# Rotary partners moved by DMA and ScalarE, and two modulation blocks summed on VectorE

## What is computed

```
mod = silu(c) @ w_mod + b_mod            # shift1, scale1, gate1, shift2, scale2, gate2
h = rms_norm(x, g1) * (1 + scale1) + shift1
(a_q, a_k, a_v, a_qi, a_ki, a_w, b_u, b_v, c_q, ..., d_q, d_k, d_v) = split_cols(h @ w_in)
q_a, k_a = rope(heads(a_q), pos), rope(heads(a_k), pos)
# rope: [x1*cos - x2*sin, x2*cos + x1*sin], x1 and x2 the halves of a 64-wide head
... four token mixers A (top-k softmax), B (gated MLP), C (forgetting), D (stick-breaking) ...
x = x + gate1 * (merged @ w_out)
h = rms_norm(x, g2) * (1 + scale2) + shift2
x = x + gate2 * conv_ffn(h)              # up, causal conv, silu * val, down
```

## Time and profile before

| | |
|---|---|
| median of 3 runs | 1100.61 us (1099.63 to 1100.64) |
| profiled execution | 1100.77 us, span of the trace 1099.0 us |
| TensorE busy | 1070.9 us (97%) |
| VectorE, ScalarE, GpSimd busy | 574.0, 601.3, 699.9 us |
| DMA | 214.95 MB, mean 196 GB/s |

### The profile page before, as it was taken

One profiled execution on the slowest core, in us unless ns is written; L12 is line 12 of the kernel. 1 busy time (PEld: TensorE's weight loads), 2 busy tenths in 40 slices (PEclk: granted clock), 3 DMA queues, 4 the chain that ended last, 5 costly groups with the idle time before them and its releaser, 6 DMA issues.

```text
span 1099.0 us, 22903 instructions
## 1 busy us (share of the span) xinstructions
PE 1070.9 (97%) x8188; PEld 979.9 (89%) x8188; DVE 574.0 (52%) x1363; ACT 601.3 (55%) x1112; POOL 699.9 (64%) x319
## 2 busy tenths in 40 slices
PE   5999999999999999999999999999999999999996
PEld 2887788898899999999998777889899999999996
DVE  4557743555267755553247576344626685555112
ACT  3564456445446665655456545554545776656542
POOL 0874545445567887778877444545557788777882
PEclk9999999999999999999999999999999999999999
DMA  9955467766654454445566546774534435444541
GB/s 358 362 212 197 186 231 281 235 232 227 199 180 159 148 183 163 153 165 180 191 210 246 209 177 229 252 255 155 189 119 154 154 132 185 176 157 153 191 166 73
DMA packets 85694, 214.95 MB, mean 196 GB/s; under 512 B 13336, under 2 KB 33376, under 8 KB 85360
## 3 DMA queue, kind: packets, MB, share of 16 engines
q1 hardware_dynamic: 85616, 213.88, 55.4%
HBM read 208.80 MB, written 5.05 MB: 195 GB/s over the span
## 4 chain that ended last, share of the span: by engine, by line
PE 85%; DVE 10%; ACT 2%; DMA 2%; issue 1%; SPq 1%; DVEq 0%; POOL 0%; ACTq 0%
PE ps L720 11%; PE ps L716 11%; PE ps L717 11%; PE ps L755 10%; PE ps L756 9%; PE ps L757 9%; PE ps L652 4%; PE ps L708 2%; PE ps L707 2%; PE ps L706 2%; PE ps L1120 2%; PE ps L646 1%; DVE scr L1770 1%; DVE hup L1690 1%; PE ps L861 1%
## 5 line engine op out<-in xcount | busy, mean ns | idle before, releaser
L596 POOL TENSOR_TENSOR wlo<-raw,whi 128x1024 fp32r<-128x1024 f32 x282 | 675.6, 2401 | 347.9 <-ACT whi L1214 290.0
L1214 ACT ACTIVATE whi<-raw 128x1024 fp32r<-128x1024 f32 x202 | 211.6, 1054 | 83.2 <-PE ps L720 62.6
L755 PE MATMUL ps<-hh,whi 128*128 128x288 f32 x816 | 250.6, 307 | 0.8 <-ACT gb L1296 0.8
L756 PE MATMUL ps<-hl,whi 128*128 128x288 f32 x816 | 241.6, 296 | 0.0
L757 PE MATMUL ps<-hh,wlo 128*128 128x288 f32 x816 | 241.3, 296 | 0.0
L755 PEld LDWEIGHTS ps<-hh,whi 128*128 128x128 f32 x816 | 153.7, 188 | 39.0 <-issue 36.2
L717 PE MATMUL ps<-ol,whi 128*128 128x290 f32 x576 | 156.9, 297 | 0.0
L716 PE MATMUL ps<-oh,whi 128*128 128x290 f32 x576 | 156.7, 297 | 0.0
L756 PEld LDWEIGHTS ps<-hl,whi 128*128 128x128 f32 x816 | 153.9, 189 | 0.2
L757 PEld LDWEIGHTS ps<-hh,wlo 128*128 128x128 f32 x816 | 153.7, 188 | 0.0
L716 PEld LDWEIGHTS ps<-oh,whi 128*128 128x128 f32 x576 | 108.9, 189 | 0.0
(11 more groups left out here) (264 smaller groups left out, 1907.0 us busy)
## 6 DMA issues: line engine op xcount, KB each, us to landing
raw<-stream SPq DMA_DIRECT2D x228, 512.0 KB, 4.2
mraw<-stream SPq DMA_DIRECT2D x40, 1024.0 KB
raw<-stream SPq DMA_DIRECT2D x88, 128.0 KB, 5.0
raw<-stream SPq DMA_DIRECT2D x24, 384.0 KB, 5.4
first<-mod_first SPq DMA_DIRECT2D x16, 512.0 KB, 11.6
raw<-stream SPq DMA_DIRECT2D x28, 256.0 KB, 5.2
o_proj<-proj SPq DMA_DIRECT2D x12, 288.0 KB
kvk<-keys_t SPq DMA_DIRECT2D x6, 512.0 KB, 6.4
```

Source lines behind the costliest of these rows:

```text
L596: nc.gpsimd.tensor_tensor(wlo[:, slot, :], raw[:, slot, :], whi[:, slot, :].bitcast(F32), ALU.subtract).then_inc(lo_ready, 1)
L755: mm(out, whi[:, slot, w], high, start=(i == 0), stop=False)
L756: mm(out, whi[:, slot, w], low, start=False, stop=False)
L1214: A(whi[:, slot, :], raw[:, slot, :], ACT.Copy).then_inc(hi_ready, 1)
```

## The change

- The swaps n = 3 to 6 leave TensorE. For each, SP issues four DMAs, which copy 32 partitions by 288 columns each from `proj` to a free slot of `gb`, the halves of each head exchanged (`move_partners`). ScalarE copies the result to PSUM bank 4, 2, 6 or 7 (`take_partner`), at the beginning of its steps t = 18, 19, 21 and 22. `rotate` is as before. In SP's list the copies stand behind piece `in_no(t) + 8` (23, 24, 25 and 26), after that piece's `load_mod` if it has one.
- TensorE's waits for the rotations change: `turn_rows` at t = 19 waits for four rotations (before: five), the logits at t = 20 for five, and the wait for all seven moves from t = 22 to t = 23.
- Two blocks of layer 1's modulation (four pairs, 4 MB) are multiplied in layer 0's down stage on VectorE. The loads stand in SP's list, one ahead of the output stage and three between down pieces, for which SP's loop is written out in the down stage of layer 0. After down tiles 1 to 4 VectorE multiplies one pair: eight instructions of 512 columns, with sums in PSUM banks 2 and 3. In layer 1 TensorE sums the partitions with four matmuls ahead of its first own pair, and layer 1 has 12 pairs instead of 16 (those at t = 32, 34, 36 and 38 are gone).

```
-SWAP_AT = {4: (0, 1, 2), 17: (3,), 18: (4,), 20: (5,), 21: (6,)}
-SWAP_BANK = (4, 3, 5, 4, 4, 4, 4)
+SWAP_AT = {4: (0, 1, 2)}
+PARTNER_AT = {18: 3, 19: 4, 21: 5, 22: 6}
+SWAP_BANK = (4, 3, 5, 4, 2, 6, 7)
+SIDE_LOADS = {8: (1,), 12: (2,), 14: (3,)}
...
+                def move_partners(n):
+                    t = ROPED[n]
+                    sp.wait_ge(bank_free[in_no(t) % 2], taken(l, in_no(t) // 2 + 1))
+                    for r in range(0, P, 64):
+                        for a, b in ((r, r + 32), (r + 32, r)):
+                            sp.dma_start(gb[a:a + 32, n, :], proj[b:b + 32, t, :]).then_inc(partner_loaded[n - ROPED_EARLY], 16)
...
                     if q in after:
                         load_mod(after[q])
+                    for n in range(ROPED_EARLY, len(ROPED)):
+                        if q == in_no(ROPED[n]) + 8:
+                            move_partners(n)
...
+                    sp.wait_ge(mod_read, upto(l, mod_read))
+                    load_side(0)
+                    out_rounds(S_DOWN)
+                    down_pairs()
...
+                def add_side_blocks():
+                    pe.wait_ge(side_turn, 8 * SIDE_BLOCKS)
+                    for g in range(4):
+                        row = 2 * (MOD_B_PAIRS // 2 - SIDE_BLOCKS + g // 2) + g % 2
+                        i = mm(ps[32 * g:32 * g + 32, MOD_BANK, :], one_pad[:, 31 - row:63 - row], side_sums[:, g // 2, g % 2, :],
+                               start=True, stop=True, skip_group_check=True)
...
-                        pe.wait_ge(roped, upto(l, roped, 5))
+                        pe.wait_ge(roped, upto(l, roped, 4))
                         turn_rows(DV, 3, v_turned)
                     if t == 20:
                         pe.wait_ge(v_tok, upto(l, v_tok, 1))
+                        pe.wait_ge(roped, upto(l, roped, 5))
                         prompt_logits(D_ROWS, 0, DQ, DK)
                     if t == 22:
-                        pe.wait_ge(roped, upto(l, roped))
                         turn_probs(D_ROWS, 0)
                         prompt_logits(D_ROWS, 1, DQ, DK)
                     if t == 23:
+                        pe.wait_ge(roped, upto(l, roped))
                         values(D_ROWS, 0)
...
+                def take_partner(n):
+                    act.wait_ge(partner_loaded[n - ROPED_EARLY], upto(l, partner_loaded[n - ROPED_EARLY]))
+                    if n == 3:
+                        act.wait_ge(vb_tok, upto(l, vb_tok))
+                    elif n == 4:
+                        act.wait_ge(scored, upto(l, scored))
+                    else:
+                        act.wait_ge(ol_ready, upto(l, ol_ready, 2))
+                    A(ps[:, SWAP_BANK[n], 0:T], gb[:, n, :], ACT.Copy).then_inc(swapped, 1)
...
+                def add_side_pair(i):
+                    dve.wait_ge(side_loaded[i % 2], 16 * (i // 2 + 1))
+                    for c in range(4):
+                        k = 4 * (i % 2) + c
+                        w = side_pair(i)[:, c // 2, c % 2 * 512:(c % 2 + 1) * 512]
+                        if k:
+                            dve.wait_ge(side_turn, 8 * (i // 2) + k)
+                        for g in range(2):
+                            total = ps[:, 2 + g, :]
+                            by = cpad[:, 32 * k + 30 + g:32 * k + 31 + g]
+                            if k == 0:
+                                s = V.tensor_scalar(total, w, by, None, ALU.mult)
+                            else:
+                                s = V.scalar_tensor_tensor(side_sums[:, i // 2 % 2, g, :] if k == KT - 1 else total, w, by, total,
+                                                           ALU.mult, ALU.add)
+                        s.then_inc(side_turn, 1)
```

More of the change, by code:

```diff
@@ L246, in encoder @@
         fal, _, n2 = place("fal", [P, FT, CC], F32R, at=proj_at + n)
-        hup, _, n3 = place("hup", [P, KT, CC], F32, at=proj_at + n + n2)
+        hup, hup_at, n3 = place("hup", [P, KT, CC], F32, at=proj_at + n + n2)
         assert n + n2 + n3 <= gates_at + gates_n - proj_at and n + n2 >= proj_n
@@ L275, in encoder @@
         conv, _, _ = place("conv", [P, 4, CC], F32, at=kv_at)
+        side_sums, _, n = place("side_sums", [P, 2, 2, 512], F32, at=hup_at)
+        assert n <= n3
+        side_w, _, _ = place("side_w", [P, 2, PIECE], F32, at=kv_at)
         lf, _, _ = place("lf", [8, T], F32)
@@ L292, in encoder @@
         shifts, _, _ = place("shifts", [P, NI, 2], F32)
+        one_pad, _, _ = place("one_pad", [P, 63], F32)
         ctx.enter_context(nc.sbuf_tensor("fence", [P, top[0] - base + 64], mybir.dt.uint8))
@@ L348, in encoder @@
         swapped = signal("swapped", 7)
+        partner_loaded = [signal(f"partner_loaded{n}", 4 * 16) for n in range(ROPED_EARLY, len(ROPED))]
         roped = signal("roped", 7)
@@ L407, in encoder @@
         y_ready = sem("y_ready")
+        side_loaded = [sem(f"side_loaded{s}") for s in range(2)]
+        side_turn = sem("side_turn")
         fin = [sem(f"final{i}") for i in range(6)]
@@ L437, in mod_pairs, with own_pairs, side_pair @@
         def mod_pairs(l):
-            return MOD_PAIRS if l + 1 < DEPTH else MOD_B_PAIRS
+            return MOD_PAIRS if l + 1 < DEPTH else own_pairs(l)
+        def own_pairs(l):
+            return MOD_B_PAIRS - (2 * SIDE_BLOCKS if l else 0)
+        def side_pair(i):
+            return side_w if i % 2 else mraw
         act_own, dve_own = sem("act_own"), sem("dve_own")
@@ L526, in _, with load_side, down_pairs, out_rounds @@
                 sp.dma_start(lfp[:], logf_past[l]).then_inc(vecs_loaded, 16)
-                def out_rounds():
-                    with sp.Fori(0, (NSTEP - S_OUT) // 4) as r:
+                def load_side(i):
+                    if i >= 2:
+                        sp.wait_ge(side_turn, 4 * (i - 1))
+                    n = MOD_B_PAIRS - 2 * SIDE_BLOCKS + i
+                    sp.dma_start(side_pair(i)[:], rounds[1, NIN // 2 + n].rearrange("s p n -> p s n")).then_inc(side_loaded[i % 2], 16)
+                def down_pairs():
+                    for q in range(S_DOWN, NSTEP, 2):
+                        sp.wait_ge(lo_ready, upto(l, lo_ready, q - 2))
+                        for j in range(2):
+                            slot = slot_for(l, q + j)
+                            sp.dma_start(raw[:, slot, :], rounds[l, (NMOD + q + 1) // 2, j]).then_inc(raw_loaded[slot], 16)
+                        if q - S_DOWN == 8:
+                            sp.wait_ge(fal_ready, upto(l, fal_ready))
+                        for i in SIDE_LOADS.get(q - S_DOWN, ()):
+                            load_side(i)
+                def out_rounds(last):
+                    with sp.Fori(0, (last - S_OUT) // 4) as r:
                         for q in (S_OUT, S_OUT + 2):
@@ L646, in turn, with mod_quad @@
                 return mm(out, in_, ident[0:k, 0:k], start=True, stop=True, is_transpose=True)
-            def mod_quad(bank, j, half, pieces):
+            def mod_quad(bank, j, half, pieces, first=True):
                 for g in range(4):
@@ L652, in mod_quad @@
                     i = mm(ps[32 * g:32 * g + 32, bank, :], cpad[:, at + 30 - 2 * j:at + 62 - 2 * j],
-                           pieces[g // 2][:, (g % 2) * 512:(g % 2 + 1) * 512], start=(j + half == 0), stop=True,
+                           pieces[g // 2][:, (g % 2) * 512:(g % 2 + 1) * 512], start=(first and j + half == 0), stop=True,
                            skip_group_check=True)
@@ L695, in mod_pair @@
                     k = n if m < 0 else m
-                    mod_quad(MOD_BANK, k // 2, k % 2, [mraw[:, i, :] for i in range(2)])
+                    mod_quad(MOD_BANK, k // 2, k % 2, [mraw[:, i, :] for i in range(2)], l == 0)
+                def add_side_blocks():
[4 more added lines that the diff above has]
+                               start=True, stop=True, skip_group_check=True)
                 def product(out, slot, wcols, terms, ready=None, before=0):
@@ L769, in swap @@
                     pe.wait_ge(bank_free[i % 2], taken(l, i // 2 + 1))
[L770 to L776, removed]
                     if t == AKI:
-                        mm(ps[0:IDX, SWAP_BANK[n], 0:T], cst[0:IDX, perm:perm + IDX], proj[0:IDX, MISC, :], start=True,
+                        mm(ps[0:IDX, SWAP_BANK[n], 0:T], cst[0:IDX, C_PI:C_PI + IDX], proj[0:IDX, MISC, :], start=True,
                            stop=True).then_inc(swapped, 1)
                         return
-                    mm(ps[:, SWAP_BANK[n], 0:T], cst[:, perm:perm + P], proj[:, t, :], start=True, stop=True).then_inc(swapped, 1)
+                    mm(ps[:, SWAP_BANK[n], 0:T], cst[:, C_PI:C_PI + P], proj[:, t, :], start=True, stop=True).then_inc(swapped, 1)
                 def index_dots(n):
@@ L1081, in _ @@
                         if mod_step(n) == t:
+                            if l and n == 0:
+                                add_side_blocks()
                             mod_pair(n)
@@ L1410, in _ @@
```

(7 more changed lines are left out.)

8 lines of the change are left out of this document (6 added, 2 removed).

## The result

The changed kernel takes 1091.74 us (median of 6 runs, 1091.06 to 1095.73) against 1100.62 us: ratio 0.9923, 95% interval 0.9912 to 0.9935. It is 8.9 us faster. The forecast was 1117.5 us, slower, with 91%; the time lies outside the range of 1108 to 1132. What came is the rival with 6%: the copies are there nearly in time.

What follows compares the result with a forecast made beforehand. TensorE, busy 97% of the span, was taken to bound the kernel. 1100.77 + 16.2 (stalls net of swaps, two layers) - 3.2 (modulation) + 3.75 (clock) = 1117.5 us, slower; range 1108 to 1132.

Steps and rivals of the forecast that it cites:

- the rival with 6%: Copies hidden, so no long waits in either layer: faster, 1088.3 us; chance 6%.
- What the copies wait for: n = 3 copies leave SP behind the 1 MB load issued at 113.97, land at 119.0; TensorE waits 3.6 us before `turn_rows`.
- a departure before 112: Sign in SP's queue that the forecast is wrong: the copies leave SP before 112.
- What is late next: Stalls ahead of the logits (5.05 us) and `turn_probs` (4.35 us); each layer loses 8.1 us net, two layers 16.2.
- The clock: TensorE's granted clock falls after long stalls, 1.25 us each; three of four falls counted over two layers, 3.75 us.
- The 5.0 that the prediction gave beside it: Upper bound of the clock loss over two layers, 4 x 1.25 us; also the term by the Trainium skill's page.
- What goes: Four swaps and two idle times leave TensorE, 4.65 us per layer; layer 1's modulation pairs go as well.
- Modulation: Layer 1 on TensorE: four pairs go, 4.26 us, four new matmuls give 1.07 back; 3.2 us gained.
- VectorE in the down stage: Eight multiplies take 5.5 us per tile in layer 0's down stage, with room for 6.5; cost nothing.
- the third rival: GpSimd holds VectorE's down-stage multiplies: up to 50 us more, some 1168 us; chance 3%.
- Others at nothing: SP's loads ahead of the output stage and between down pieces, and three small memsets at the start, cost nothing.

Runs made afterwards that it cites:

- sums first: Changed kernel with copies two pieces earlier in SP's queue, and VectorE's softmax sums moved ahead of rotation n = 5: 1093.52 us, ratio 0.9943.
- the partners: Changed kernel without its modulation part, so layer 1 multiplies all sixteen pairs on TensorE again: 1095.33 us, ratio 0.9954 to the kernel before.
- own banks: Kernel before, its four swaps still matmuls but through banks 4, 2, 6 and 7 with the changed kernel's waits, no modulation on VectorE: 1094.93 us, ratio 0.9950.
- late copies: Changed kernel with each of the four sets of copies two pieces later in SP's queue: 1124.85 us, ratio 1.0217 to the kernel before.

## Why the prediction was wrong

1. **What the copies wait for** failed, in its first lines: the load "and only behind it the four copies for n = 3". The load's time was right (113.97 against 113.98), the copies' place in the queue was not; they left at 105.47, behind the load before (the prediction names a departure before 112 as the sign that it is wrong). Everything behind hung on it, and at the real place TensorE had no wait ahead of `turn_rows` and 0.19 to 1.30 us ahead of the other two, instead of 3.6 to 5.05. With the copies put where the prediction had them, the same kernel took 1124.85 us, in the range of 1108 to 1132 and 7 us above the value.
2. **What is late next** was right as a mechanism, shown by that run: three stalls, 12.69 us for 13.0 reckoned. That the sum is so near is luck. Counted as the prediction counts, from the pair at t = 16 to the start of `turn_probs`, it is 43.3 and 42.1 us in the two layers where 38.2 was reckoned, 9.0 us later together. 4.6 of it is the landing, mis-sized in all four places (5.95 to 6.46 us for 5.0); 2.4 is the clock, since the load of pair 7 left 3.15 and 2.78 us behind the logits' start, not 1.77; the rest, 2.0, is spread over the other steps.
3. **The clock** was mis-sized. The prediction left out what is lost behind the first stall, as hidden in the second. That was so: 2.4 and 1.35 us were lost there, and the second stall came out at 3.44 and 3.87 instead of 5.05. Behind the second stall 2.4 count (the load of pair 7, just named), behind the third 1.25 and 1.41 up to the pair at t = 22: 5.05 us against 3.75, and 1.7 more up to the pair at t = 24 (8.69 and 9.82 us, 8.4 before). The 5.0 that the prediction gave beside it was nearer. In the changed kernel the term is nothing, since no wait in that stretch is longer than 1.3 us and its clock stayed at 1.00.
4. **What goes** was right in its sum: 31.75 - 27.0 = 4.7 us a layer for 4.65 reckoned. Two errors cancel there: a swap takes 0.48 us and not 0.58, since a gap between groups stays when the swap goes, and the two idle times were worth 2.80 and not 2.33. The stretch shrank by 3.68 and 2.57 only, because new waits came ahead of the logits and of `turn_probs` (0.82 and 1.92 by the brackets).
5. **Modulation**, 3.2 us gained. Seven traces with this part give it directly (sums first is left out, since its new wait falls in). From layer 1's pair at t = 24 (676.03 before, 671.24 after) to the end of the span they are 2.2 to 4.8 us shorter, 3.7 on average for 4.26 reckoned; the two traces without it are 0.1 longer and 0.1 shorter. From a pair late in layer 0 (308.63 before, 305.18 after) to one early in layer 1 (606.07 and 603.89) the seven are 1.1 to 1.5 us longer, 1.3 on average, of which 0.9 are the four new matmuls (593.00 to 593.88 after; 1.07 reckoned). So about 2.5 net, and from 0.9 to 3.5 in single traces. The run times say 1.9 alone, about 3.3 beside the partners and 0.5 beside the swaps in own banks, and can't tell better.
6. **VectorE in the down stage** was right. VectorE's timeline there, one tile with multiplies:

```profile
536.37 0.47 DVE L1696 TENSOR_TENSOR ps<-ps,work 128x288 f32<-128x288 f32 x1 [6.53 <-ACT work L1297]
536.92 0.64 DVE L1830 SCALAR_TENSOR_TENSOR ol<-ps,norm_a,oh 128x256 fp32r<-128x256 f32 x2
537.48 1.40 DVE L2270 TENSOR_SCALAR ps<-mraw,cpad 128x512 f32<-128x512 f32 x2
538.91 4.31 DVE L2272 SCALAR_TENSOR_TENSOR ps<-mraw,cpad,ps 128x512 f32<-128x512 f32 x6
543.13 0.64 DVE L1810 SCALAR_TENSOR_TENSOR x<-ps,mod,x 128x256 f32<-128x256 f32 x2
```

Eight multiplies take 5.65 us (537.48 to 543.13; 5.5 reckoned). GpSimd was at work without a gap from 536.02 to 545.52 and didn't hold them, so the third rival falls. That agrees with what the Trainium skill, page "SBUF — State Buffer", section "Who interferes with whom", says of instructions with one SBUF input, and the rotation's operation with two, held for 1.94 and 2.42 us above, is the other side of it. One input in SBUF is no warrant by itself: the `score<-score` of the late copies, which has one, took 1.84 us beside GpSimd instead of 0.23. Why it was held and the multiplies were not, no run shows.
7. **Others at nothing**: SP did stand in the loads for VectorE. The waits of its queue in the changed kernel:

```profile
SPq L551 <- DVE ps L2272: 7.4, 1, 7.4
SPq L551 <- DVE side_sums L2272: 7.3, 1, 7.3
SPq L551 <- PE ps L708: 5.6, 1, 5.6
```

It cost at most what point 5 leaves, 1.3 - 0.9 = 0.4 us. That the pieces held ahead covered the rest is likely, but no run shows it.

What stays open: why the kernel without copies but with modulation was not nearer to the changed one in run times, what the own banks give without the later wait, and what the clock takes in an execution of the median length.

## What to carry to other kernels

Where the forecast hangs on a place in a queue, work that place out from the numbers of the program, slot by slot, and check it against one that the trace shows, before anything is priced: here a wrong slot number turned the sign, while the chain worked out behind it held in kind, each stall within about a third. Undo what makes work wait (one bank for four swaps, a wait that stands a tile earlier than it must) before moving the work to other engines: these two gave most of the gain, and the route through DMA and ScalarE gave back, in waits of its own, half or more of the 1.9 us per layer that the matmuls had cost. A queue with a blocking load in it has a cliff: two pieces earlier was worth 1 us, two later cost 33.

## What was not expected of the hardware

A copy of 36 KB from SBUF to SBUF held SP for 0.59 us per issue, as much as the `raw` pieces of 512 KB issued between the sets (0.58 and 0.59; 0.46 in pairs elsewhere), and landed 3.9 to 4.7 us after its issue behind a 1 MB load, in layer 1 4.0 to 5.0; the DMA answer for the first set in layer 0:

```profile
L580 SPq DMA_DIRECT2D gb<-proj x4: 590/591/624, 105.5 to 107.4; - x4
...
DMA to landing us min/median/max: 3.9/4.1/4.7
```

In the changed kernel's stretch, waits of TensorE up to 1.3 us left its clock at 1.00; with the late copies, each of the six stalls of 3.44 to 4.80 us was followed by a fall.
